# Spreading one projection tile thinner over a block inverse, and more evenly over a chain of state hops

## The reference, cut to what matters

```python
def _even_layer(x, norm_g, w_in, w_out, ...):
    h = _rmsnorm(x, norm_g)
    z = (h @ w_in).astype(jnp.float32)
    za, zb, gate = jnp.split(z, [3 * A_WIDTH, 3 * A_WIDTH + RW_SLAB], axis=-1)
    qa, fa, ia = jnp.split(za, 3, axis=-1)
    zb = zb + (_shift(zb) - zb) * mu
    ...
    y = jnp.concatenate([oa, ob], axis=-1) * jax.nn.silu(gate)
    return y.astype(x.dtype) @ w_out

# _rwkv7, per head and token; computed by the kernel in chunks of 64 tokens
def step(state, inp):
    rt, wt, kt, vt, kkt, at = inp
    sa = jnp.einsum('bhvk,bhk->bhv', state, -kkt)
    state = state * wt[:, :, None, :] + sa[..., None] * (kkt * at)[:, :, None, :] + vt[..., None] * kt[:, :, None, :]
    return state, jnp.einsum('bhvk,bhk->bhv', state, rt)
```

## Time and profile before

| | |
|---|---|
| Median of 3 runs | 1252.65 us |
| Lowest, highest | 1251.61, 1259.87 us |
| The profiled execution's own time | 1252.65 us |
| Its span in the trace | 1250.7 us |
| TensorE busy | 1157.0 us, 93% of the span |
| Mean granted TensorE clock | 0.977 of full speed |
| TensorE instructions (matmuls) | 12058, and as many weight loads |

### The profile page before, as it was taken

How to read it: one execution, slowest core, us unless ns; L and a number is a source line. 1 busy time by engine, 2 the same in 40 slices (tenths; PEclk the granted TensorE clock), 3 DMA queues, 4 the chain that set the end, 5 groups by cost and what they waited for, 6 DMA issues and landing times.

```text
span 1250.7 us, 31010 instructions
## 1 busy us (share of the span) xinstructions
PE 1157.0 (93%) x12058; PEld 915.2 (73%) x12058; DVE 760.6 (61%) x1344; ACT 441.1 (35%) x827; POOL 617.5 (49%) x584
## 2 busy tenths in 40 slices
PE   2899999999999999999995799997899999989995
PEld 1678778877787777877774588785677777768873
DVE  7656575675656856567555410648468686866547
ACT  4343343343423435234333410324234434352223
POOL 3644452443534434344251167775647475739761
PEclk9999999999999999999998899998899999999997
DMA  5221121211211212112120223332222221213321
GB/s 205 69 71 59 47 68 46 62 53 50 64 46 60 62 37 67 56 52 70 37 77 27 85 78 118 93 93 59 84 69 84 68 84 59 88 55 93 93 84 67
DMA packets 46744, 88.69 MB, mean 71 GB/s; under 512 B 5808, under 2 KB 6832, under 8 KB 46384
## 3 DMA queue, kind: packets, MB, share of 16 engines
q1 hardware_dynamic: 44352, 82.37, 21.6%
q10 hardware_dynamic: 2288, 4.72, 1.1%
HBM read 84.97 MB, written 2.10 MB: 70 GB/s over the span
## 4 chain that ended last, share of the span: by engine, by line
PE 77%; DVE 15%; issue 3%; ACT 3%; DMA 1%; SPq 0%; DVEq 0%; ACTq 0%
PE psum L328 75%; DVE mix L1392 3%; ACT mix L977 2%; DVE mix L1416 2%; PE psum L914 1%; DVE mix L1918 1%; DVE mix L1836 1%; DVE mix L1847 1%; DVE h_split L1396 1%; PE psum L451 1%; DVE mix L1910 1%; DVE mix L1901 1%; DVE mix L1916 1%; DVE y L1922 1%; DMA mix<-xT 1%
## 5 line engine op out<-in xcount | busy, mean ns | idle before, releaser
L328 PE MATMUL psum<-h_split,w_hi 128*128 128x512 f32 x2320 | 753.9, 406 | 28.7 <-DVE mix L1494 11.1
L328 PEld LDWEIGHTS psum<-h_split,w_hi 128*128 128x128 f32 x2320 | 427.0, 191 | 137.8 <-issue 43.0
L311 POOL TENSOR_SCALAR w_hi<-w_raw 128x512 fp32r<-128x512 f32 x290 | 209.8, 723 | 583.0 <-PE psum L328 431.6
L328 PE MATMUL psum<-h_split,w_lo 128*128 128x512 f32 x1160 | 458.4, 395 | 0.0
L313 POOL TENSOR_TENSOR w_lo<-w_raw,w_hi 128x512 fp32r<-128x512 f32 x290 | 408.2, 1408 | 24.2
L328 PEld LDWEIGHTS psum<-mix 64*64 64x64 f32 (+3 forms) x8256 | 231.8, 138 | 81.1 <-issue 54.2
L328 PE MATMUL psum<-mix 64*64 64x64 f32 (+5 forms) x8256 | 274.5, 236 | 15.5 <-DVE mix L1392 4.4
L977 ACT ACTIVATE mix<-psum 128x512 f32<-128x512 f32 (+4 forms) x292 | 140.8, 495 | 410.6 <-PE psum L328 266.5
L328 PEld LDWEIGHTS psum<-h_split,w_lo 128*128 128x128 f32 x1160 | 220.7, 190 | 48.4
L977 ACT ACTIVATE mix<-mix 128x512 f32<-128x512 f32 (+2 forms) x266 | 137.8, 548 | 187.0 <-DVE mix L1819 72.3
L1487 DVE COPY_PREDICATED mix<-mask,psum 128x128 f32<-128x128 uint8 (+1 forms) x192 | 82.9, 469 | 52.8 <-PE psum L328 39.9
(11 more groups left out here) (115 smaller groups left out, 635.1 us busy)
## 6 DMA issues: line engine op xcount, KB each, us to landing
w_raw<-wall SPq DMA_DIRECT2D x290, 256.0 KB, 2.6
mix<-xT SPq DMA_DIRECT2D x4, 512.0 KB, 5.4
mix<-xT ACTq DMA_DIRECT2D x1, 2048.0 KB, 7.9
out<-mix SPq DMA_DIRECT2D x8, 256.0 KB, 2.1
mix<-mask_f SPq DMA_DIRECT2D x1, 1728.0 KB, 10.8
mix<-pT ACTq DMA_DIRECT2D x2, 512.0 KB, 3.5
mix<-lru_w ACTq DMA_DIRECT2D x4, 256.0 KB, 3.1
mix<-w2a ACTq DMA_DIRECT2D x16, 32.0 KB, 2.2
```

The source lines that it names most:

```text
L311: pool.tensor_scalar(w_hi[:, slot, :, :], w_raw[:, slot, :], 1.0, 0.0, ALU.mult, ALU.add).then_inc(sem["w_hi"], 1)
L328: return pe.matmul(o, lhsT, rhs, start=start, stop=stop, skip_group_check=True)
```

## The change

In rounds 1 to 7 on TensorE, the inverse gets four single chunks of tile 3 in place of ten chunks of tiles 3 and 4: chunk 0 and chunk 1 between `inverse_pt` and `inverse_n` of levels 2 and 3, chunk 2 behind `inverse_n` of level 4, chunk 3 behind `inverse_pt` of level 5. Nothing stands any more behind level 1. Chunks 4 and 5 of tile 3 go before `transitions`, 6 and 7 behind `state_sums`. Each of the six hops is then followed by two chunks: all of tile 4, and half of tile 5. `level(0)` and `level(1)` move behind them. ACT's sigmoid of tile 3 moves from before `solved_rows` to between `level_copies` 2 and 3, and DVE's `gated(i, 3)` from before `solved_rows` to between `hop_add` 5 and `hop_state` 5. Round 0 keeps its work, with the chunks of tiles 4 and 5 in larger pieces; round 8 keeps its order. No matmul, load, copy or DMA is added or taken away, apart from one wait on `rw_tok` on TensorE.

```diff
@@ TensorE, even_round, if pair:
                     key_products(r, 1)
-                    pe.wait_ge(sem["rw_tok"], count("rw_tok", r, 0))
-                    filler(3, 0, 2)
                     for lvl in range(2, 5):
                         inverse_pt(r, lvl, 0)
                         inverse_pt(r, lvl, 1)
                         if lvl == 4:
                             value_rows(r)
+                        elif head:
+                            t(3, lvl - 2, lvl - 1)
                         inverse_n(r, lvl, 0)
                         inverse_n(r, lvl, 1)
                         if lvl < 4:
                             token_rows(r, lvl, head)
-                        filler(3, 2 * lvl - 2, 2 * lvl)
+                        elif head:
+                            t(3, 2, 3)
                     inverse_pt(r, 5, 0)
                     inverse_pt(r, 5, 1)
-                    filler(4, 0, 2)
+                    if head:
+                        t(3, 3, 4)
                     inverse_last(r, 0)
...
                     solved_rows(r, 1)
-                else:
-                    t(4, 0, 2)
-                t(4, 2, 4)
+                if head and not first:
+                    t(3, 4, 6)
                 embedding(2)
                 if pair:
                     transitions(r)
                     output_sums(r, False)
                     state_sums(r, False)
-                t(4, 4, 6)
+                if head and not first:
+                    t(3, 6, KC)
                 embedding(3)
+                for c in range(1, 5):
+                    if pair:
+                        hop(r, c)
+                    t(4, 2 * c - 2, 2 * c)
                 if pair:
-                    hop(r, 1)
-                t(4, 6, 7)
+                    hop(r, 5)
+                t(5, 0, 2)
                 if pair:
-                    hop(r, 2)
-                t(4, 7, KC)
-                t(5, 0, 1)
-                if pair:
-                    hop(r, 3)
-                t(5, 1, 2)
-                if pair:
-                    hop(r, 4)
+                    hop(r, 6)
+                t(5, 2, 4)
                 level(0)
                 level(1)
-                if pair:
-                    hop(r, 5)
-                t(5, 2, 3)
-                if pair:
-                    hop(r, 6)
-                t(5, 3, 4)
                 if pair:
                     state_outputs(r)
@@ ScalarE
-                    if head:
-                        tile_done(i, 3)
-                        act.wait_ge(sem["free0"], freed(i, 2))
-                        f(sig_a, bank[1][:, :], ACT.Sigmoid).then_inc(sem["sig_gb"], 1)
                     solved_rows(r)
...
                     level_copies(i, 2)
+                    if pair:
+                        tile_done(i, 3)
+                        act.wait_ge(sem["free0"], freed(i, 2))
+                        f(sig_a, bank[1][:, :], ACT.Sigmoid).then_inc(sem["sig_gb"], 1)
                     level_copies(i, 3)
@@ VectorE
-                    if head:
-                        gated(i, 3, "sig_gb", sig_a, g_b)
                     solved_rows(r)
...
                     hop_add(r, 5)
+                    if head:
+                        gated(i, 3, "sig_gb", sig_a, g_b)
                     hop_state(r, 5)
```

More of the change, by code:

```diff
@@ L681, in t @@
                         part_tile(i, j, start, end, 0 if first and j == 3 else None)
-                def filler(j, start, end):
-                    if head:
-                        part_tile(i, j, start, end)
                 def level(lvl):
```

## The result

The changed kernel takes 1264.09 us (median of 9 runs, 1261.4 to 1266.36) against 1252.19 us for the kernel before in 9 runs: a ratio of 1.0088, 95% interval 1.0072 to 1.0104. The forecast was 1265.7 us in a range of 1251 to 1275. The profiled execution of the changed kernel took 1266.54 us, its span is 1264.6 us; both are 13.9 us above those of the kernel before.

The account below looks back on a forecast made before the run. TensorE's own work was taken to bound rounds 1 to 7. Per round, +2.2 fetch, -0.1 old gap, -0.2 hop 5, +0.15 bank 1, -0.2 changes give +1.85; times 7, +13.0 on 1252.65: 1265.7 us, range 1251 to 1275.

Parts of the forecast that it names:

- The bound was TensorE's queue: Rounds 1 to 7: the time is TensorE's own work, with less than 4 us in all left to win.
- The fetch term: Inverse, rounds 1 to 7: denser small matmuls outrun the instruction packets, so TensorE waits 2.2 us a round, bounds 0 to 4.3.
- The figure of 4.1 us between packets: TensorE's instruction queue: a packet is usable at the soonest 4.1 us after TensorE has entered the one before.
- the packet in hand: Inverse: the first packet is already there, so 2.1 of the 4.3 us a round is not paid.
- The rule of the hidden fetch: Instruction queue: the next page is fetched during the current one, so no fetch term; 1251 us as a rival, chance 0.20.
- Old gaps: Rounds 1 to 7: the one old 0.7 us gap goes, -0.1 us a round spread over seven.
- Hops and bank 1: Hop 5's wait for its state goes, -0.2 us a round; t(5, 0) waits for the moved gate product, +0.15.
- the -0.2 for changes: Each round: one of five places where tile and small matmuls meet in the inverse goes, `level(0)` joins state outputs: -0.2 us.
- Round 0 adds nothing: Round 0, outside the seven changed rounds: no time added to the total.
- Round 8 adds nothing: Round 8, outside the seven changed rounds: no time added to the total.

Follow-up runs that it names:

- the control: The kernel before, with chunk 0 of tile 3 issued three times more behind level 1 in rounds 1 to 7: 1267.76 us against 1253.42 (1.0123).

## Why the prediction was right, step by step

**The bound was TensorE's queue.** Right: the control prices added work at 14.3 of 14.5 us, and the 13.9 us by which the profiled execution grew are 10.3 of idle TensorE and 3.6 of busy.

**The fetch term, +2.2 us a round.** Right in mechanism and nearly in size. Of the seven stretches from products to hop 1, before, the shortest takes 29.90 us (rounds 2 and 6); less six chunks and one change that is 25.6. After the change they take 26.9 to 28.9, 28.0 on average: 2.4 us a round. Each round pays differently (1.3 to 3.3), as the edges fall. Of the 2.4 the stops at the packets' boundaries are 2.0, counted between the loads (15.2 - 1.0 us over seven rounds), against the 2.2 of the sum; what the other 0.4 is, these runs do not say. In the waits, which go by the matmuls, "issue" came to 11.6 us and not to the some 15 forecast.

The figure of 4.1 us between packets, read off four gaps of round 8, carried the sum, the 1280 us of the kernel without chunks and the 1252 to 1256 us of the one with eight. It holds as an average (4.08 over 48 pairs) and not as "at the soonest": neighbouring gaps end as little as 3.5 us apart (3.6 in the changed kernel, where the prediction allowed no nearer than about 4). Single boundaries are crossed 2.5 us after the one before without a stop, as in round 6 of the changed kernel just ahead of its first gap (522.44 and 524.96 us): the packet in hand.

**The rule of the hidden fetch.** The Trainium skill (Runtime: NRT & Kernel Launch, section Instruction fetch mechanics) gives pages of 256 instructions; the remainder that all 109 gaps share agrees with that. It also calls the cost of crossing from one to the next mostly hidden. The trace of the kernel before agrees for its rounds 1 to 7 (one gap of 0.7 us), and those of the kernels with few chunks in the inverse do not (11.6 and 20.5 us of "issue").

**Old gaps, -0.1.** Mis-sized if all that varies between the rounds is counted: 30.17 - 29.90 = 0.27 us a round. Stops at packet boundaries are 1.0 of these 1.9 us in all; the rest is not explained.

**Hops and bank 1, -0.2 + 0.15 and part of the -0.2 for changes.** The mechanisms of the two waits were right, and both runs on DVE's order confirm them. The wait for bank 1 was 0.23 us and not 0.15, hop 5's 0.21. The stretch from hop 1 on grew by 4.18 us for 4.14 us of chunks, so nothing was gained there, where I had a few tenths.

The hops in the changed kernel, all engines, beside the earlier trace rows:

```profile
548.23 1.29 POOL L313 TENSOR_TENSOR w_lo<-w_raw,w_hi 128x512 fp32r<-128x512 f32 x1
...
548.32 1.28 DVE L1382 SCALAR_TENSOR_TENSOR mix<-mix 128x64 f32<-128x64 f32 x1
...
549.17 0.33 PE L328 MATMUL psum<-mix 128*128 128x64 f32 x2
...
550.78 0.33 PE L328 MATMUL psum<-mix 128*128 128x64 f32 x2
...
553.83 0.68 DVE L1484 TENSOR_TENSOR mix<-psum,mix 128x512 f32<-128x512 f32 x1
...
554.57 0.73 PE L328 MATMUL psum<-h_split,w_hi 128*128 128x512 f32 x2 [0.23 <-DVE mix L1484]
```

The hops stand 1.61 us apart, as worked out. The gate product starts at 553.83, and TensorE waits for its end until 554.57.

**Round 0 adds nothing: wrong by 0.7 us.** `level(0)` and `level(1)` now stand right ahead of `hg_values`, and in round 0 there are no state outputs between. TensorE waits for the first mask, once:

```profile
65.62 0.63 PE L612 MATMUL psum<-fconst,mix 128*128 128x128 f32 x4 [0.58 <-DVE mix L1477]
```

**Round 8 adds nothing: the -2.0 us is not the change's.** Its TensorE program is the same and starts at the same instruction count, but its "issue" gaps sum to 2.0 us in this execution against 3.5 before, which is 1.5 of the 2.0. Ahead of round 8 the changed kernel lost 1.1 us the other way. After TensorE's 9.6 us idle there, the granted clock of the next matmuls was 0.60, against 0.74 in the same place before:

```profile
682.11:688.69 6.58, 5.40 (x12) 3.77 (x13) 0.00 (x0) 1.09 (x2) 0.89 (x2) 0.60 0.00 0
```

(a window of the changed kernel, columns as in the earlier trace rows). Both are differences between executions that these runs do not explain. Sum by rounds: 7 x (2.4 - 0.3 + 0.04) + 0.7 is 15.7 us; the profiled pair shows 13.9, the medians 11.9. So the closeness of the forecast's 13.0 to these is in part luck: round 8 and the spread between executions took back what the forecast had too low in rounds 0 to 7.

## What to carry to other kernels

Where an engine runs many small instructions, count them beside the time. Here a stretch in which 256 of TensorE's instructions after another run in less than about 4.1 us on average waits for the next packet, however well every semaphore is covered. Long matmuls placed among the short ones cost less there than their own time (0.9 us for 2.8, in the stretch with four chunks more), up to the point where the pace is met: 3.3 us for 126 pairs of load and matmul stalled, 3.7 a little, 4.4 hardly. So tiles should go to the dense stretch first, and to a latency-bound chain only with what is left. Before spreading work over such a chain, see whether the late instruction only stands behind one that could wait.

## What the runs showed of the hardware that was not expected

- All 109 unexplained gaps of nine traces end at one remainder by 256 of TensorE's instruction count, 1.2 to 1.7 us after a packet of 16,384 bytes has landed on the instruction queue.
- Two waits on semaphores share one instruction: 128 added waits made 64.
- The same TensorE program lost 8.6 us and 11.6 us to missing instructions in two executions that differ only in the place of one DVE operation. The packets ahead of the 109 gaps took 0.9 to 2.0 us each; what makes that vary was not tried.
- DVE's 128x64 operation on two SBUF operands took 1.28 us in place of 0.28 when it began while GpSimd's 1.29 us split was running (548.32 above). In the changed kernel's trace all eight that began in such a split took 0.77 to 1.28 us and ended 0.08 us after it; the 25 that began while GpSimd was idle took 0.28 to 0.29. TensorE did not wait for the operation at 548.32, with two chunks behind each hop. No run varied it on purpose.
